# Fourteen stripes for a head, scatters at an even pace between gathers, dots that lag behind the heads

## The chip, the cores and the metric

The kernel runs on one core of one Trainium2 chip. The metric is the time of one execution in device microseconds (us); less is better.

## The reference, cut to what matters

One step of a decoder layer for 512 prompt tokens and 64 sample tokens, width 2048. After three branches (pooling, attention, cross-attention) and their merge comes the part that matters here, a feed-forward layer of 16384 experts of which each token uses 128:

```python
q = (xt @ w_q).reshape(n, PEER_HEADS, 2, PEER_HALF)
s = jnp.einsum('nhpd,hpkd->nhpk', q, subkeys)
s_top, i_top = lax.top_k(s, PEER_TOPK)
cand = s_top[:, :, 0, :, None] + s_top[:, :, 1, None, :]
cand_idx = i_top[:, :, 0, :, None] * PEER_N_KEYS + i_top[:, :, 1, None, :]
best, sel = lax.top_k(cand.reshape(n, PEER_HEADS, PEER_TOPK * PEER_TOPK), PEER_TOPK)
eidx = jnp.take_along_axis(cand_idx.reshape(n, PEER_HEADS, -1), sel, axis=-1)
gate = jax.nn.softmax(best, axis=-1)
...
a = jax.nn.gelu(jnp.einsum('ted,td->te', u[ib], xb), approximate=False)
return jnp.einsum('te,ted->td', gb * a, v[ib])
```

There are 8 heads (PEER_HEADS), 16 experts for each token and head (PEER_TOPK), 128 keys on each side (PEER_N_KEYS). `u` and `v` are the arrays `peer_u` and `peer_v`, 16384 rows of 2048.

## The kernel before

The kernel is a sequence of stages with a barrier between them. The change touches the one that reads `peer_u` (semaphores `q6`). The 576 tokens are five blocks: four of 128, one of 64. Blocks 1 to 3 (384 tokens) are treated densely: TensorE multiplies them by all of `peer_u`, in 128 stripes of 128 experts (kind "u"), ScalarE takes Gelu of each stripe's result and stores it in DRAM. Which experts a token has chosen is brought in by scatters: for each token, head and place, its gate goes to the place of (expert, token) in `routes_scratch`, which was filled with zeros earlier. Blocks 0 and 4 are treated sparsely: for each place, a gather brings 128 rows of `peer_u` (8 KB each, 1.05 MB a gather) into one of three buffers (`ring`), and VectorE forms the dot product of each row with its token in one instruction (`dot`, L1523). There are 192 gathers and 192 dots, and 384 scatters of 128 single values.

The queries of the heads come from 16 stripes of `w_pq` (kind "q", two a head, all 576 tokens in two column halves). So the stage has 144 stripes. They go in groups: the first GROUP x 8 stripes are 8 groups of two "q" and GROUP - 2 "u" stripes, and the rest are "u".

What each engine does for a stripe s:

- SyncE loads its two halves (512 KB each) into `w_raw`, four buffers, each when VectorE is done with the one before in that buffer.
- ScalarE rounds each half to fp32r (`w_hi`, L130). VectorE forms the rest (`w_lo`, L139); two such instructions a stripe are called its splits. There are four such pairs of buffers, two stripes of them.
- TensorE multiplies three times for each 128 x 128 block: hi by hi, lo by hi, hi by lo. A "u" stripe has 48 matmuls of 384 columns, a "q" stripe 96 of 288. After the third stripe of a group it also computes the head's scores.
- ScalarE drains the result (L1353 for "u", L1345 for "q"), so the starts of its drains mark the ends of stripes. After the fourth stripe of a group it copies the scores out.
- VectorE, after its splits of stripe s, does the steps that `plan` has for s, then dots up to `dots_by(s)`.

The steps of a head, all on VectorE: five `list` steps (top 16 of each side, a block each), `candidates`, `choose` (top 16 of the candidates), `shift`, `unpack`, two `look_up`, `number` (the expert's number), `weigh` (gates, and the copy `gate_sums` for the scatters), and `add_same(h)`. The last adds to a gate the gates of the same expert in earlier heads, in up to three parts of three heads each: a comparison (L1489), a product (L1491), a sum (L1493) and an addition (L1494). When it is done, `s_head` rises, and GpSimd may scatter and gather for that head. Nearly every step is a chain whose links wait for each other through `s_tk`.

VectorE's order is written out: HEAD_STEPS says in which stripe, counted from the head's first, a step stands (FIRST_STEPS for head 0). Before, with GROUP = 10, steps of head h reach into group h + 1: `add_same` is in the same stripe as the next head's `list1`.

GpSimd issues all gathers (L1325) and scatters (L1313) in one order: ahead of gather q it issues scatters until `scatters_before(q)` are out. Gather q waits until dot q - 3 is done (three buffers) and at every 24th for its head; the first scatter of a head waits for the head and for all scatters before it to land. ScalarE moves the sample tokens' part of `eidx` and `gate` to other partitions after each head (`move_sample`), and the gathers for sample tokens wait for that.

The stage ends when all dots, stores and scatters are done. Then the next stage multiplies by `peer_v`.

## Time and profile before

| what | us |
|---|---|
| median of three executions | 4664.35 (4663.63 to 4670.29) |
| the profiled execution | 4673.19 |
| its span | 4671.6 |
| matmul, busy | 4274.8 (92%) |
| VectorE, busy | 2644.5 (57%) |
| ScalarE, busy | 1249.9 (27%) |
| GpSimd, busy | 1715.3 (37%) |
| granted TensorE clock, mean | 0.954 |

The span reaches from the first to the last instruction of the profile, and all times of rows are counted from its start. Busy time of GpSimd is that in which it makes the descriptors of its DMAs, not that of the transfers. Shares are means over the stages; the stage of the change lies between 2051 and 3554 us.

### The profile page before, as it was taken

How to read it: one execution, taken by the hardware profiler on the slowest of the kernel's cores; microseconds unless marked ns; L12 is line 12 of the kernel's file. 1: busy time of each engine (PE TensorE's matmuls, PEld its weight loads, DVE VectorE, ACT ScalarE, POOL GpSimd, SP SyncE). 2: the span in 40 equal slices, each digit the busy share in tenths (PEclk: the TensorE clock that was granted, in tenths of full speed). 3: DMA queues.
4: the chain of work that ended last, by engine and by line, in shares of the span. 5: the costliest groups of instructions: out<-in, count | busy, mean ns of one | idle time of the engine just before them, and what ended most of it. 6: DMA issues, size and time to landing. Idle time of an engine off the chain costs nothing. (4 is left out here: it accounts for less than half of the span.)

```text
span 4671.6 us, 76860 instructions
## 1 busy us (share of the span) xinstructions
PE 4274.8 (92%) x28688; PEld 4161.8 (89%) x28688; DVE 2644.5 (57%) x3611; ACT 1249.9 (27%) x1625; POOL 1715.3 (37%) x1305
## 2 busy tenths in 40 slices
PE   5999999999698898969999998888886999999997
PEld 5999999999466798969999997888886999999997
DVE  4222111111322452246888889666666988888887
ACT  4111133333112221132333322222222333332332
POOL 0000100000111000002555544887785767666772
PEclk8999999999798999989999998999998999999998
DMA  4822332322476333135666655998887999999996
GB/s 158 314 81 81 124 107 104 107 104 90 142 253 256 139 133 129 63 123 178 245 245 222 216 215 217 331 335 317 319 314 289 372 361 357 359 356 362 358 355 258
DMA packets 279277, 1061.58 MB, mean 227 GB/s; under 512 B 43635, under 2 KB 94195, under 8 KB 225971
## 3 DMA queue, kind: packets, MB, share of 16 engines
q1 hardware_dynamic: 165490, 522.72, 31.1%
q0 software_dynamic: 93728, 510.53, 28.9%
q10 hardware_dynamic: 19936, 26.78, 1.6%
q8 instruction: 67, 1.10, 0.1%
q14 instruction: 56, 0.45, 0.0%
HBM read 977.47 MB, written 81.33 MB: 227 GB/s over the span
## 5 line engine op out<-in xcount | busy, mean ns | idle before, releaser
L139 DVE TENSOR_TENSOR w_lo<-w_raw,w_hi 128x1024 fp32r<-128x1024 f32 x498 | 600.8, 1230 | 1058.9 <-ACT w_hi L130 1048.7
L130 ACT ACTIVATE w_hi<-w_raw 128x1024 fp32r<-128x1024 f32 x498 | 519.2, 1059 | 1252.3 <-PE acc L167 760.0
L1313 POOL DMA_INDIRECT routes_scratch<-gate_sums,route x384 | 560.9, 1461 | 272.5 <-DVE gate_sums L1477 124.7
L167 PE MATMUL acc<-x_hi,w_hi 128*128 128x288 f32 x2592 | 558.0, 297 | 17.8 <-DVE w_lo L139 17.6
L167 PE MATMUL acc<-x_lo,w_hi 128*128 128x288 f32 x2592 | 557.3, 297 | 0.0
L167 PE MATMUL acc<-x_hi,w_lo 128*128 128x288 f32 x2592 | 556.9, 297 | 0.1
L167 PE MATMUL acc<-h_hi,w_hi 128*128 128x384 f32 (+1 forms) x1280 | 411.5, 338 | 98.2 <-DVE w_lo L139 96.4
L167 PEld LDWEIGHTS acc<-x_hi,w_hi 128*128 128x128 f32 x2592 | 419.8, 190 | 18.8 <-DVE w_lo L139 14.3
L167 PE MATMUL acc<-h_hi,w_hi_peeru 128*128 128x384 f32 (+1 forms) x1280 | 408.3, 335 | 30.6 <-DVE w_lo_peeru L139 30.6
L167 PEld LDWEIGHTS acc<-x_hi,w_lo 128*128 128x128 f32 x2592 | 419.7, 190 | 0.2 <-issue 0.2
L167 PEld LDWEIGHTS acc<-x_lo,w_hi 128*128 128x128 f32 x2592 | 419.9, 190 | 0.0
L167 PE MATMUL acc<-h_lo,w_hi 128*128 128x384 f32 (+1 forms) x1280 | 408.2, 335 | 0.0
L167 PE MATMUL acc<-h_hi,w_lo 128*128 128x384 f32 (+1 forms) x1280 | 407.3, 335 | 0.4 <-issue 0.4
L167 PE MATMUL acc<-h_lo,w_hi_peeru 128*128 128x384 f32 (+1 forms) x1280 | 406.0, 333 | 0.0
L167 PE MATMUL acc<-h_hi,w_lo_peeru 128*128 128x384 f32 (+1 forms) x1280 | 405.8, 333 | 0.0
L1796 PE MATMUL acc<-tile_hi,w_hi 128*128 128x384 f32 x1024 | 342.9, 335 | 45.8 <-DVE w_lo L139 45.8
L1523 DVE SCALAR_TENSOR_TENSOR ring<-ring,h_row 128x2048 f32<-128x2048 f32 x128 | 292.5, 2287 | 138.9 <-DMA ring<-in_peer_u,eidx 124.2
L130 ACT ACTIVATE w_hi_peeru<-w_raw 128x1024 fp32r<-128x1024 f32 x272 | 278.7, 1054 | 325.0 <-PE acc L1796 262.8
L139 DVE TENSOR_TENSOR w_lo_peeru<-w_raw,w_hi_peeru 128x1024 fp32r<-128x1024 f32 x272 | 322.1, 1224 | 68.6 <-ACT w_hi_peeru L130 50.1
L1796 PE MATMUL acc<-tile_hi,w_hi_peeru 128*128 128x384 f32 x1024 | 346.8, 339 | 0.2 <-DVE w_lo_peeru L139 0.2
L1796 PE MATMUL acc<-tile_lo,w_hi_peeru 128*128 128x384 f32 x1024 | 346.7, 339 | 0.0
L1796 PE MATMUL acc<-tile_hi,w_lo_peeru 128*128 128x384 f32 x1024 | 346.6, 338 | 0.0
(321 smaller groups left out, 8500.5 us busy)
## 6 DMA issues: line engine op xcount, KB each, us to landing
w_raw<-in_w_peer_u SPq DMA_DIRECT2D x256, 512.0 KB
w_raw<-in_w_peer_v SPq DMA_DIRECT2D x256, 512.0 KB
w_raw<-in_w_gate SPq DMA_DIRECT2D x96, 512.0 KB, 3.7
w_raw<-in_w_z SPq DMA_DIRECT2D x66, 512.0 KB, 3.3
k_ring<-in_cache_k SPq DMA_DIRECT2D x64, 512.0 KB, 5.0
v_ring<-in_cache_v POOLq DMA_DIRECT2D x64, 512.0 KB, 6.3
routes_scratch<-zero POOLq DMA_DIRECT2D x8, 3072.0 KB, 50.1
activations_scratch<-a_out ACTq DMA_DIRECT2D x128, 192.0 KB
```

Source lines behind the costliest of these rows:

```text
L130: nc.scalar.activation(slot(q, j)[0], raw[:, j % 4, :], ACT.Copy).then_inc(q["hi"], 1)
L139: nc.vector.tensor_tensor(lo, raw[:, j % 4, :], hi.bitcast(F32), ALU.subtract).then_inc(q["lo"], 1)
L167: last = nc.tensor.matmul(dst, l_, r_[:, cc, c0:c0 + cn], start=(cc == first and p_ == 0), stop=(cc == last_c and p_ == 2))
L1313: pool.indirect_dma_start(route_dram, bass.IndirectOffsetOnAxis(ap=route[:, b, n:n + 1], axis=0), gsum[:, h % SUMS, b - 1, n % PTOP:n % PT ...
L1523: nc.vector.scalar_tensor_tensor(out=ring[:, r, :], in0=ring[:, r, :], scalar=1.0, in1=hrow[:] if r < 2 else hrow_s[:], op0=ALU.mult, op1= ...
L1796: last = nc.tensor.matmul(acc[:, s, h, 0:ND], l_, r_[:, t_, :], start=(c == 0 and p_ == 0), stop=(c == GRP - 1 and p_ == 2))
```

## The change

A group has fourteen stripes instead of ten, so the 16 "q" stripes spread over 112 stripes instead of 80. HEAD_STEPS is laid out anew: `choose` goes block by block in five steps (before: three steps for blocks 0 and 1, 2 and 3, and 4), and `add_same` becomes three steps, one a part, `sums0` and `sums1` in stripe 16 and `sums2` in stripe 17 from the head's first, which are the third and fourth of the next group, where no `list` step stands. `s_head` then rises by an instruction of its own behind `sums2`. The dots start at stripe 16 instead of 14 and go at 1 a stripe to stripe 34, 7/5 a stripe to stripe 118, and 11/5 a stripe from there. In a stripe, half of its dots (rounded down) stand ahead of the head's steps. Ahead of gather q there are 9q/4 scatters, up to all 384; before, 3 a gather and 4 ahead of the first, to gather 70, and then 17/12 a gather.

```diff
-        GROUP = 10
+        GROUP = 14
...
-                      10: ("choose1",), 11: ("choose2", "shift"), 12: ("unpack", "look_up0"), 13: ("look_up1",), 14: ("number", "weigh"), 15: ("add_same",)}
...
+                      10: ("choose1", "choose2"), 11: ("choose3", "choose4", "shift"), 12: ("unpack",), 13: ("look_up0",), 14: ("look_up1",),
+                      15: ("number", "weigh"), 16: ("sums0", "sums1"), 17: ("sums2",)}
...
-        move_at = {s + 1: h for s in plan for h, name in plan[s] if name == ("add_same" if h else "weigh")}
-        LAST_STEP = GROUP * (PH - 1) + 14
+        move_at = {s + 1: h for s in plan for h, name in plan[s] if name == ("sums2" if h else "weigh")}
+        LAST_FREE = GROUP * (PH - 1) + 20
 
         def dots_by(s):
 
-            return 0 if s < 14 else min(NGAT, s - 13 if s < LAST_STEP else LAST_STEP - 13 + 2 * (s - LAST_STEP))
+            if s < 16:
+                return 0
+            return s - 15 if s <= 34 else min(NGAT, 19 + 7 * (min(s, LAST_FREE) - 34) // 5 + 11 * max(0, s - LAST_FREE) // 5)
 
         def scatters_before(q):
 
-            return 4 + 3 * q if q < 70 else min(NSCT, 214 + (q - 70) * 170 // 120)
+            return min(NSCT, 9 * q // 4)
...
-                def choose(blocks):
-                    link(sixteen([(cand[:, b, :], rest_c[:, n, :], best[:, b, :], sel[:, b, :]) for n, b in enumerate(blocks)]))
+                def choose(b):
+                    link(sixteen([(cand[:, b, :], rest_c[:, b % 2, :], best[:, b, :], sel[:, b, :])]))
...
-                def add_same(h):
-
-                    dve.wait_ge(s_lst, NBLK * (h + 1) + (h < PH - 1))
-                    for h0 in range(0, h, 3):
+                def add_same(h, part_no):
+
+                    h0 = 3 * part_no
+                    if h0 == 0 and h < PH - 1:
+                        dve.wait_ge(s_lst, NBLK * (h + 1))
+                    if h0 < h:
...
-                        last = nc.vector.tensor_tensor(gsum[:, h % SUMS], gsum[:, h % SUMS], psum_[:], ALU.add)
-                        if h0 + 3 < h:
-                            link(last)
-                    last.then_inc(s_head, 1)
+                        link(nc.vector.tensor_tensor(gsum[:, h % SUMS], gsum[:, h % SUMS], psum_[:], ALU.add))
+                    if part_no == 2:
+                        dve.sem_inc(s_head, 1)
...
                 for s in range(NS_):
                     split_lo(dve, s // 2, s % 2, q6)
+                    if s == 13:
+                        dve.wait_ge(s_hmv, 16)
+                    early = dots_by(s - 1) + (dots_by(s) - dots_by(s - 1)) // 2
+                    for q in range(dots_by(s - 1), early):
+                        dot(q)
                     for h, name in plan.get(s, ()):
                         step(h, name)
-                    if s == 13:
-                        dve.wait_ge(s_hmv, 16)
-                    for q in range(dots_by(s - 1), dots_by(s)):
+                    for q in range(early, dots_by(s)):
                         dot(q)
```

## Rows read from the trace of the kernel before

**Rows 1.** Windows cut at drains: bounds and length, busy time (instructions), clock, DMA share, GB/s.
```profile
2067.20:2149.50 82.30, 82.30 (x502) 82.30 (x501) 44.70 (x153) 28.11 (x35) 0.00 (x0) 1.00 0.40 132
2149.50:2849.40 699.90, 673.60 (x4173) 671.79 (x4172) 584.49 (x1326) 202.35 (x249) 351.68 (x280) 0.98 0.63 226
2247.30:2342.30 95.00, 95.00 (x598) 95.00 (x597) 80.37 (x193) 29.27 (x36) 51.22 (x40) 1.00 0.67 236
2437.40:2534.50 97.10, 95.29 (x598) 94.97 (x597) 84.56 (x193) 29.29 (x36) 51.63 (x41) 1.00 0.65 233
...
2742.50:2849.40 106.90, 97.02 (x597) 96.70 (x597) 93.00 (x197) 29.29 (x36) 47.91 (x40) 0.95 0.59 211
2849.40:2891.40 42.00, 42.00 (x243) 42.00 (x242) 37.65 (x55) 15.38 (x19) 19.29 (x13) 1.00 0.72 259
2891.40:3508.70 617.30, 531.10 (x2832) 522.08 (x2830) 417.04 (x364) 145.56 (x176) 491.44 (x284) 0.93 0.86 313
```

**Rows 2.** Waits, 2891.4 to 3508.7 us: us in total, times, longest.
```profile
DVE ring L1523 <- DMA ring<-in_peer_u,eidx: 121.9, 52, 7.9
...
DVE ring L1523 <- DMA ring<-in_peer_u,expert_sample: 60.3, 25, 5.7
```

**Rows 3.** GpSimd's groups by line, 2891.4 to 3508.7: busy us, mean ns | idle before.
```profile
L1313 POOL DMA_INDIRECT routes_scratch<-gate_sums,route x166 | 288.7, 1739 | 64.4 <-issue 57.4 <-DMA routes_scratch<-gate_sums,route 7.0
L1325 POOL DMA_INDIRECT ring<-in_peer_u,eidx x78 | 132.8, 1702 | 29.9 <-issue 22.6 <-DVE ring L1523 7.3
L1325 POOL DMA_INDIRECT ring<-in_peer_u,expert_sample x40 | 74.9, 1872 | 31.9 <-DVE ring L1523 20.3 <-issue 11.6
```

**Rows 4.** The same groups, 2240.9 to 2843.1 us.
```profile
L1313 POOL DMA_INDIRECT routes_scratch<-gate_sums,route x180 | 229.6, 1276 | 72.2 <-issue 53.6 <-DMA routes_scratch<-gate_sums,route 18.6
L1325 POOL DMA_INDIRECT ring<-in_peer_u,eidx x40 | 52.0, 1301 | 148.4 <-DVE ring L1523 145.6 <-issue 2.7
L1325 POOL DMA_INDIRECT ring<-in_peer_u,expert_sample x21 | 27.7, 1318 | 76.6 <-DVE ring L1523 75.4 <-issue 1.2
```

**Rows 5.** Timelines of GpSimd and VectorE, 2928 to 2950 us: start, us, instruction.
```profile
2931.30 2.73 POOL L1325 DMA_INDIRECT ring<-in_peer_u,eidx  x1 [0.30 <-issue]
2934.34 1.99 POOL L1313 DMA_INDIRECT routes_scratch<-gate_sums,route  x1 [0.30 <-issue]
...
2944.19 0.98 POOL L1325 DMA_INDIRECT ring<-in_peer_u,expert_sample  x1 [0.30 <-issue]
...
2930.90 2.29 DVE L1523 SCALAR_TENSOR_TENSOR ring<-ring,h_row 128x2048 f32<-128x2048 f32 x1 [3.31 <-DMA ring<-in_peer_u,eidx]
...
2933.11 2.36 DVE L139 TENSOR_TENSOR w_lo<-w_raw,w_hi 128x1024 fp32r<-128x1024 f32 x2
...
2944.35 2.29 DVE L1523 SCALAR_TENSOR_TENSOR ring<-ring,h_row 128x2048 f32<-128x2048 f32 x1 [1.31 <-DMA ring<-in_peer_u,eidx]
```

**Rows 6.** Timeline of VectorE over one stripe with a list and a dot.
```profile
2812.49 2.35 DVE L139 TENSOR_TENSOR w_lo<-w_raw,w_hi 128x1024 fp32r<-128x1024 f32 x2
...
2817.51 2.27 DVE L1523 SCALAR_TENSOR_TENSOR ring<-ring,g_row 128x2048 f32<-128x2048 f32 x1
...
2819.70 2.35 DVE L139 TENSOR_TENSOR w_lo_peeru<-w_raw,w_hi_peeru 128x1024 fp32r<-128x1024 f32 x2
```

**Rows 7.** VectorE's groups by line and form, 2040 to 3560 us.
```profile
L1489 DVE TENSOR_TENSOR same_expert<-eid_f,eidx 128x2304 f32<-128x2304 f32 x7 | 17.9, 2552 | 0.1
...
L1489 DVE TENSOR_TENSOR same_expert<-eid_f,eidx 128x768 f32<-128x768 f32 x3 | 2.9, 956 | 0.1
```

**Rows 8.** Window of VectorE over five stripes from `candidates` to `look_up1`: length, busy.
```profile
2834.80:2879.60 44.80, 39.75 (x78) 1.00 0.73 262
```

**Rows 9.** A window of the next stage, columns as in rows 1.
```profile
3700.00:3800.00 100.00, 100.00 (x573) 100.00 (x573) 89.70 (x80) 30.08 (x36) 68.23 (x51) 1.00 0.95 369
```

**Rows 10.** Timelines of VectorE, ScalarE and SyncE's queue at the end of the stage.
```profile
3515.44 2.29 DVE L1523 SCALAR_TENSOR_TENSOR ring<-ring,g_row 128x2048 f32<-128x2048 f32 x1 [1.07 <-DMA ring<-in_peer_u,expert_sample]
...
3508.69 0.49 ACT L1353 ACTIVATE a_out<-acc 128x384 f32<-128x384 f32 x1 [7.99 <-PE acc L167]
...
3519.47 0.40 SPq L1629 DMA_DIRECT2D out_t<-activations_scratch  x1
```

More of the change, by code:

```diff
@@ L1249, in build @@
         HEAD_STEPS = {4: ("list0",), 5: ("list1",), 6: ("list2",), 7: ("list3",), 8: ("list4",), 9: ("candidates", "choose0"),
-                      10: ("choose1",), 11: ("choose2", "shift"), 12: ("unpack", "look_up0"), 13: ("look_up1",), 14: ("number", "weigh"), 15: ("add_same",)}
-        FIRST_STEPS = {4: ("list0", "list1"), 5: ("list2", "list3"), 6: ("list4", "candidates"), 7: ("choose0",), 8: ("choose1",),
-                       9: ("choose2", "shift"), 10: ("unpack", "look_up0"), 11: ("look_up1", "number"), 12: ("weigh",)}
+                      10: ("choose1", "choose2"), 11: ("choose3", "choose4", "shift"), 12: ("unpack",), 13: ("look_up0",), 14: ("look_up1",),
+                      15: ("number", "weigh"), 16: ("sums0", "sums1"), 17: ("sums2",)}
+        FIRST_STEPS = {4: ("list0", "list1"), 5: ("list2", "list3"), 6: ("list4", "candidates"), 7: ("choose0", "choose1"),
+                       8: ("choose2", "choose3"), 9: ("choose4", "shift"), 10: ("unpack", "look_up0"), 11: ("look_up1", "number"), 12: ("weigh",)}
         plan = {}
@@ L1504, in step @@
                     elif name.startswith("choose"):
-                        choose(((0, 1), (2, 3), (4,))[int(name[6:])])
+                        choose(int(name[6:]))
                     elif name == "shift":
@@ L1516, in step @@
                     else:
-                        add_same(h)
+                        add_same(h, int(name[4:]))
                 def dot(q):
```

## The prediction

> **What bounds the kernel now.** I first asked the windows where TensorE is not full. Only the stage of the diff matters: it runs from about 2051 us to the first matmul of the next stage at 3554 us, and in it the windows are cut at the drains of single stripes [rows 1]. From 2067.2 to 2149.5 us nine stripes pass (one of kind "q", eight of kind "u", one set of scores) and TensorE is 100% busy; the five "u" stripes of 2849.4 to 2891.4 us take 42.0 us. So a "u" stripe costs 8.4 us, and a group of ten (two "q", eight "u", one set of scores) 95.0 us, as in the full window from 2247.3 us. Everything above that is lost time, and it stands in two places. The seven groups of 2149.5 to 2849.4 us take 699.9 us where 665.0 would do: 34.9 us. Their windows one by one (two that repeat the pattern aren't shown, 102.6 and 105.4 us) put 32.0 of it on the sums of heads 3 to 6 (2.1, 7.6, 10.4, 11.9) and nearly all the rest, 2.8, on the first. The last 59 stripes take 617.3 us where 495.6 would do: 121.7 us. Together 156.6 us, the most that a better order of this stage can give back.
>
> What ends last in each? In the last 59 stripes the waits [rows 2] say that VectorE stood 182.2 us for rows of `peer_u` to land, while GpSimd, which orders those transfers, stood only 27.6 us for a free buffer [rows 3]: GpSimd never catches up, its orders are the bottleneck. The groups by line give 284 orders (118 gathers, 166 scatters), busy 496.4 us with 126.2 us between them: 2.19 us an order, 2.07 without the 34.6 us in which it waited for a dot or a landing. In the early part [rows 4] 241 orders take 309.3 us, 1.28 us each, and 0.30 us stands between two that follow on each other: 1.58. The timelines of both engines [rows 5] show why one work has two prices. An order issued while VectorE is idle, as at 2944.19 us, takes 0.98 us. That of 2931.30 us takes 2.73: VectorE's dot ended at 2933.19 and the order 0.84 us behind it. That of 2934.34 met two splits that ended at 2935.47 and was done 0.86 us later. So an order waits for the end of a dot or split. The 0.98 us and the 0.30 us make a floor of 1.28 us.
>
> In heads 3 to 6 the loss is VectorE's. A stripe with one split pair, one list and one dot takes it 7.2 us, from 2812.49 to 2819.70 [rows 6]: 2.3 the pair, 2.2 the dot, 2.7 the list. `add_same` adds three steps of 2.55 us and some small change, 8.0 us, for three earlier heads, and 3.2 for one (three of 0.96) [rows 7]; I take 5.6 between them for two. All of it stands in the stripe of `list1`: 12.8 us for head 2 (loss 0.1), 15.2 for head 3 (2.1), 18.4, 20.8, 23.2 for heads 4 to 6 (7.6, 10.4, 11.9). About 13 us pass unseen since splits are ahead of TensorE; head 7's stripe (no list, but a second dot and three parts: 26 us) lies in the last window, and by the same slope I put 15 of its 121.7 us down to it.
>
> **The change, part by part.** *Work.* Nothing is removed: 192 gathers, 384 scatters and all vector steps remain, in another order. `choose` goes block by block, five chains of four links in place of three; the rows show no cost beyond some 0.1 us a link, under 1 us a head, hidden in stripes of 8.4 us. The added semaphore step on VectorE is an order of its sequencer. `move_sample` moves to the stripe after `sums2` with both its transfers and the sample gathers that wait for them; the first gather of a head is due later than that.
>
> *Pace.* Before, 71 dots were done at stripe 84 and then two a stripe. After: one a stripe to 34 (19 dots), 7/5 to 118 (136), then 11/5 (191 at stripe 143). A group of 14 costs TensorE 95.0 + 4 x 8.4 = 128.6 us, 9.19 a stripe.
>
> *Waits on heads.* Scatters of head h start before gather 22, 44, 65, 86, 107, 129, 150 (h = 1 to 7), which the dots let go at stripes 35, 51, 66, 81, 96, 112, 124; the heads are done at 31, 45, 59, 73, 87, 101, 115. Four to eleven stripes of margin: nothing, and a head must be 34 us late before GpSimd stands.
>
> *Sums.* `sums0` and `sums1` stand in the third stripe of the next group, behind two "q" stripes. 82.3 - 8 x 8.4 = 15.1 us is one "q" and the scores, 95.0 - 8 x 8.4 = 27.8 two and the scores: a "q" stripe takes TensorE 12.7 us, 4.3 more than "u", so about 17.3 us pass unseen there. With the dots of those stripes VectorE needs 17.9 us (head 4, two dots), 18.1 (head 5), 20.5 (head 6): 1 us and 4 us lost. Head 7 has no "q" stripes after it: 22.7 us against 13, by the losses above some 11, and 2 for the look-ups just before. Sum 18 us, where it was 32.0 + 15.
>
> *Stripes 34 to 118.* Each wants 1.4 x 3.25 = 4.55 orders. At the early 1.58 us that is 7.2 us of 9.19 (loss 0), at 2.07 it is 9.4, at 2.19 10.0, a loss of 0.8 x 84 = 65 us. VectorE: five stripes of choosing and look-ups are 39.75 us busy [rows 8], less five of (2.3 + 2.2), 17.3; with five lists of 2.7 that is 31 us over ten "u" stripes; with 1.4 dots and the splits 8.5 us a stripe against 8.4. So it has no room to wait for a gather, but the ring holds three rows, the head steps between dots are mostly short, and the "q" stripes give some 8 us a group back. I take 15 us, nearer the early row since its mix of steps is the same; ends 0 and 65.
>
> *Stripes 118 to 134.* Gathers 139 to 170 come with the last 72 scatters: 104 orders in the 134.4 us that 16 stripes need. Before, a gather took 617.3 / 118 = 5.23 us, of which 2.41 x 1.28 = 3.08 is the floor; the other 2.15 is held up by a dot and half a pair of splits (3.5 us of VectorE): 61% of it. After, a gather has 3.39 us of dot and splits beside it, 2.07 held up, and 3.25 x 1.28 = 4.16: 6.23 us, times 32 is 199 us. With 5 us for the last landing (an estimate) the loss is 70 us. Ends: 0 (104 x 1.28 = 133 us) and 98 (2.19 an order).
>
> *Stripes 134 to 144.* One order a gather, but 2.2 x 1.05 (128 rows of 2048 f32) + 1.05 (weights) + 0.2 = 3.55 MB a stripe; at the 369 GB/s of the next stage [rows 9] 9.6 us against 8.4. 10 us; ends 0 and 29 (at the 313 GB/s of the last window, [rows 1]).
>
> *The end.* Before, the last drain is at 3508.7, VectorE's last dots stand for rows until 3517.7, and the next stage's first load goes out at 3519.5 [rows 10]. After, three dots and no scatter are left in place of five: 6 us less (0 to 8); the last activation still has to be stored.
>
> *Sum.* Lost after: 2.8 + 18 + 15 + 70 + 10 = 115.8 us against 156.6: 40.8 us gained, with the end 47. The profiled execution took 4673.2 us (span 4671.6), 8.8 above the median of 4664.35; taken off the median, 4617 us.
>
> A rule to weigh here: the Trainium skill, SBUF — State Buffer, Who interferes with whom, says that a VectorE instruction with two SBUF inputs and a GpSimd one that reads SBUF lock each other out, and that issue order decides who waits. The first half agrees with [rows 5]. By the second, a dot or split that comes up while an order is under way would wait for it, half of its 0.98 us on average; with two such meetings a stripe that is 1 us a stripe from 34 to 118, where VectorE has none to spare, so some 80 us in place of 15. The trace does not bear it out: the dot of 2944.35, begun 0.16 us after an order, took its usual 2.29 [rows 5].
>
> **The rivals.** *Slower:* orders have the late price throughout, because 1.4 dots a stripe lay a dot or split over most of them. One price p for both stretches costs (4.55p - 9.19) x 84 + 104p + 5 - 134.4, which with the other 30.8 us passes the old 156.6 and the 6 of the end from p = 2.13 us an order. At 2.07 it gives 4637, at 2.19 some 4690. For it: 2.19 is what the late rows show. Against: that has 34.7 us of waits in it, and in the early rows the orders fall among lists.
>
> *VectorE is full* in stripes 34 to 118, so a dot's wait for its row goes to the end. Before, 119 late dots waited 1.5 us each. At 0.6 us for 117 dots, in ten of 14 stripes, 50 us in place of 15: 4652; at 0.75, 4662, no change. For it: 8.5 against 8.4 us. Against: before, early dots had their rows at once. *Orders hold up dots,* the mutual lock: each meeting costs VectorE half an order, 84 us in place of 15: 4686; against it stands the dot of 2944.35 [rows 5]. It is the second half of the rule in that section of SBUF — State Buffer of the Trainium skill.
>
> *Scatters spread out cost little:* while VectorE stands for a row, orders run at the floor. At 1.6 us an order the dense stretch loses 37 us and the earlier none: 68 in all, 4570; at the floor 4532.
>
> *The change does nothing:* the late stretch is paced by bytes, 313 GB/s there [rows 1]. Against: 369 with TensorE full in the next stage [rows 9]. 4664.
>
> **How the numbers follow.** Forecast (4580 to 4645): 0.57. Much faster, around 4550: 0.14. VectorE full, around 4655: 0.12. Slower by dear orders, 4675 to 4690: 0.11; by orders that hold up dots: 0.02. Nothing: 0.04. 0.2% is 9.3 us, about what a measurement of this kernel tells from no change. Faster by more: 0.57 + 0.14 + 0.04 of the VectorE case = 0.75; within: 0.09; slower: 0.16. The range leaves out the far half of the fast and of the slow cases, 4565 to 4675; the forecast's own is 4590 to 4645.
>
> **What would show it.** Right: groups of 14 near 129 us up to head 5 and 5 us or less over it at head 6; a loss of some 13 us behind stripe 114; then sixteen stripes that take about 200 us with VectorE waiting for rows, GpSimd hardly ever; then ten of about 9.5 us; drains end near 3468. Wrong: groups of 135 us or more with waits for rows in them; orders above 2.1 us from stripe 34 on; or the dense stretch at TensorE's pace. The weakest number is the 70 us, since it extends a share of held-up time to a density of scatters that no row shows.

## The result and the profile after

The changed kernel takes **4593.09 us**, the median of 4 runs (4578.19 to 4604.84), against 4664.82 (4663.63 to 4670.29) for the kernel before on the same chip: ratio 0.9848, 95% interval 0.983 to 0.9866. That is 71.7 us off the median where 47 were forecast. The profiled run is the slowest of the four (4604.84 us, span 4603.3), and against the profiled run of before it is 68.4 us shorter, so the traces are compared on those 68 us: 2.0 because the stage starts earlier (first drain at 2065.2 us, not 2067.2; nothing ahead of it was edited), 60.3 inside the stage (1381.2 us from first to last drain, not 1441.5), 7.6 at its end, and 1.6 given back in the rest of the program.

The windows of the changed kernel, cut at the drains of stripes 0, 34, 97, 110, 118, 134 and 143, are the answer to [rows 1]. Columns as there.

```profile
2065.20:2379.50 314.30, 314.30 (x1934) 314.30 (x1933) 201.66 (x471) 96.37 (x119) 80.39 (x70) 1.00 0.60 205
2379.50:2953.00 573.50, 573.50 (x3490) 573.50 (x3489) 524.56 (x991) 177.62 (x216) 447.26 (x280) 1.00 0.84 292
2953.00:3081.10 128.10, 123.00 (x742) 122.81 (x742) 117.03 (x218) 36.85 (x46) 98.02 (x63) 0.97 0.80 281
3081.10:3163.80 82.70, 69.98 (x386) 69.67 (x385) 71.33 (x66) 19.99 (x25) 64.09 (x38) 0.92 0.77 268
3163.80:3363.90 200.10, 152.18 (x768) 148.40 (x766) 110.31 (x97) 39.94 (x48) 162.12 (x108) 0.89 0.80 270
3363.90:3446.40 82.50, 77.77 (x432) 77.14 (x432) 67.20 (x61) 20.93 (x25) 28.36 (x19) 0.98 0.96 374
```

TensorE is busy for the whole length of the first two: in 97 stripes the head steps, and in the last 63 of them 1.4 dots and 3.15 scatters a stripe, cost it nothing. What is lost stands in the last four. A "u" stripe is 8.4 us, so 16 take 134.4 and nine 75.6, and the table compares each stretch with the terms of the prediction.

| stretch | us lost, forecast | us lost, measured |
|---|---|---|
| first group | 2.8 | 0 |
| sums of heads 1 to 6 | 5 (1 and 4) | 7.8, all of it head 6 |
| head 7, behind stripe 114 | 13 | 15.6 |
| waits in stripes 34 to 118 | 15 | 0 apart from head 6's row |
| stripes 118 to 134 | 70 | 65.7 (200.1 - 134.4) |
| stripes 134 to 143 | 10 | 6.9 (82.5 - 75.6) |
| sum, where before it was 156.6 | 115.8 | 96.0 |

In the dense stretch, 3163.8 to 3363.9 us, the waits of VectorE answer to [rows 2] (us in total, times, longest):

```profile
DVE ring L1527 <- DMA ring<-in_peer_u,eidx: 51.4, 16, 6.7
...
DVE ring L1527 <- DMA ring<-in_peer_u,expert_sample: 38.9, 10, 7.3
```

and GpSimd's groups by line over the same stretch to [rows 3]:

```profile
L1316 POOL DMA_INDIRECT routes_scratch<-gate_sums,route x74 | 110.7, 1495 | 27.1 <-issue 22.3 <-DMA routes_scratch<-gate_sums,route 4.8
L1328 POOL DMA_INDIRECT ring<-in_peer_u,eidx x23 | 32.7, 1421 | 7.0 <-issue 7.0
L1328 POOL DMA_INDIRECT ring<-in_peer_u,expert_sample x11 | 19.3, 1753 | 3.4 <-issue 3.4
```

VectorE stands 90.3 us for rows, and GpSimd, which orders them, never once for a dot: its idle time is all issue and 4.8 us of a landing. 108 orders in 200.1 us are 1.85 us each; 34 of them are gathers, 5.89 us each (6.23 forecast), of which 1.28 x 108 / 34 = 4.07 is the floor and 1.82 is held up (2.07 forecast). The timelines of GpSimd and of VectorE in that stretch show the holding up as [rows 5] did:

```profile
3270.59 0.97 POOL L1316 DMA_INDIRECT routes_scratch<-gate_sums,route  x1 [0.30 <-issue]
3271.86 2.88 POOL L1328 DMA_INDIRECT ring<-in_peer_u,eidx  x1 [0.30 <-issue]
```

```profile
3271.59 2.29 DVE L1527 SCALAR_TENSOR_TENSOR ring<-ring,g_row 128x2048 f32<-128x2048 f32 x1 [3.44 <-DMA ring<-in_peer_u,expert_sample]
```

The order at 3270.59 us met an idle VectorE and took 0.97 us. The next met the dot that ran to 3273.88, and was done at 3274.74, 0.86 behind it.

Of the 65.7 us TensorE stands 47.9. In the other 17.8 it works, but slower: its 768 matmuls are busy 152.2 us at a granted clock of 0.89, where the same number takes 134.4 at 1.00. After a wait of 9.59 us they begin 0.32 us apart, in the full stretches 0.17 to 0.18:

```profile
3287.53 0.68 PE L167 MATMUL acc<-h_hi,w_hi_peeru 128*128 128x384 f32 x1 [9.59 <-DVE w_lo_peeru L139]
3288.01 0.52 PE L167 MATMUL acc<-h_lo,w_hi_peeru 128*128 128x384 f32 x1
```

The granted clock over 3286.5 to 3298.8 us is 0.72, so part of that time is at 1.2 GHz and part at 2.4. As GpSimd never waits for VectorE or TensorE here, this is how TensorE's loss is made up and not a second cause of the stretch's length.

In the last nine intervals the picture turns round:

```profile
L1328 POOL DMA_INDIRECT ring<-in_peer_u,eidx x12 | 17.0, 1419 | 31.6 <-DVE ring L1527 31.3 <-issue 0.3
L1328 POOL DMA_INDIRECT ring<-in_peer_u,expert_sample x7 | 11.3, 1618 | 18.2 <-DVE ring L1527 18.2
```

Here GpSimd is idle 49.5 of 82.5 us for want of a free buffer, and the DMA engines are busy 0.96 of the time at 374 GB/s (windows above). That points to bytes, but does not show that they set the pace: e1 below moves 406 GB/s with the same gathers and weights. These 49.5 us next to a stretch in which GpSimd is the bottleneck are what the later experiments try to use.

The end of the stage answers to [rows 10]: the last dot, the last drain and the next stage's first load.

```profile
3445.84 2.29 DVE L1527 SCALAR_TENSOR_TENSOR ring<-ring,g_row 128x2048 f32<-128x2048 f32 x1 [2.96 <-DMA ring<-in_peer_u,expert_sample]
3446.41 0.49 ACT L1356 ACTIVATE a_out<-acc 128x384 f32<-128x384 f32 x1 [7.99 <-PE acc L167]
...
3449.90 0.40 SPq L1636 DMA_DIRECT2D out_t<-activations_scratch  x1
```

The dots now end 2 us behind the last drain and no longer 9, so the load goes out 3.5 us behind it, where it was 10.8. That is the gain at the end: the next stage's first matmul stands 38.1 us behind the last drain, where it was 45.8.

### The profile page after: what moved, and what is told of

It is laid out like the page before. It is cut to its first block and busy times, and to the rows that moved or that the text cites. A ratio compares the mean times of both kernels' runs of the same rounds, so it can differ in the third digit from the quotient of the medians.

```text
span 4603.3 us, 76657 instructions
## 1 busy us (share of the span) xinstructions
PE 4257.1 (92%) x28688; PEld 4150.7 (90%) x28688; DVE 2650.1 (58%) x3611; ACT 1250.6 (27%) x1625; POOL 1737.1 (38%) x1305
## 5 line engine op out<-in xcount | busy, mean ns | idle before, releaser
L1316 POOL DMA_INDIRECT routes_scratch<-gate_sums,route x384 | 584.1, 1521 | 145.1 <-issue 114.9
L167 PE MATMUL acc<-x_hi,w_hi 128*128 128x288 f32 x2592 | 557.5, 297 | 18.6 <-DVE w_lo L139 18.6
L167 PE MATMUL acc<-h_hi,w_hi 128*128 128x384 f32 (+1 forms) x1280 | 400.9, 330 | 30.5 <-DVE w_lo L139 30.5
L1803 PE MATMUL acc<-tile_hi,w_lo 128*128 128x384 f32 x1024 | 342.7, 335 | 0.0
```

The lines of the kernel that those rows point to most:

```text
L167: last = nc.tensor.matmul(dst, l_, r_[:, cc, c0:c0 + cn], start=(cc == first and p_ == 0), stop=(cc == last_c and p_ == 2))
L1316: pool.indirect_dma_start(route_dram, bass.IndirectOffsetOnAxis(ap=route[:, b, n:n + 1], axis=0), gsum[:, h % SUMS, b - 1, n % PTOP:n % PT ...
L1803: last = nc.tensor.matmul(acc[:, s, h, 0:ND], l_, r_[:, t_, :], start=(c == 0 and p_ == 0), stop=(c == GRP - 1 and p_ == 2))
```

## The experiments

Losses are worked out as above, stretch by stretch, from the drains of each profiled run. They carry the comparison better than whole spans do: the first drain of the stage moved between 2055.1 and 2067.2 us over the profiled runs, though no kernel here edits anything ahead of it. "The change" is the changed kernel; its 96.0 us are the measure.

**e1: the dense stretch without its scatters.**

```diff
-        NGAT, NSCT = NEXP + HC, 3 * NEXP
+        NGAT, NSCT = NEXP + HC, 3 * NEXP - 72
```

> The changed kernel without its last 72 scatters (their gates never reach the routes, so that part of the output is left out); the gathers and dots stay. Theory (the dense stretch of stripes 118 to 134 is set by the number of GpSimd's orders): with one order a gather it runs like stripes 134 to 143 do now, 82.5 us for nine, 9.2 us each, so 16 stripes take about 147 us in place of 200, and the time falls by about 50 us to some 4540 us. Rival (the stretch is set by bytes, or by VectorE and its dots): the scatters are only bystanders, the stretch keeps 180 us or more and the time stays within 15 us of 4593.

Measured: 4538.27 us (4520.91 to 4542.34), ratio 0.9735 (0.9719 to 0.9751). Stripes 118 to 134 and 134 to 143:

```profile
3147.80:3285.30 137.50, 134.78 (x770) 134.15 (x769) 113.63 (x101) 40.03 (x49) 54.84 (x37) 1.00 1.01 406
3285.30:3364.00 78.70, 75.75 (x432) 75.11 (x430) 63.42 (x57) 20.59 (x25) 29.14 (x18) 1.00 0.96 377
```

65.7 us of loss become 3.1, in the same stretch with the same gathers, dots and weights. The rate rises from 270 to 406 GB/s, so the bytes did not pace it. VectorE's waits for rows fall from 90.3 to 24.1 us, and GpSimd, which never stood for a dot, now stands 80.7 us for free buffers. So the scatters make the loss; that it is their orders, and not their transfers, e2 shows. The profiled run is the fastest of its four, 17 us below their median; by the medians this kernel is 55 us faster than the change.

**e2: dots with one SBUF input.**

```diff
-                    nc.vector.scalar_tensor_tensor(out=ring[:, r, :], in0=ring[:, r, :], scalar=1.0, in1=hrow[:] if r < 2 else hrow_s[:],
-                                                   op0=ALU.mult, op1=ALU.mult, accum_out=dots[:, c:c + 1]).then_inc(s_used, 1)
+                    nc.vector.reduce_sum(dots[:, c:c + 1], ring[:, r, :], AX.X).then_inc(s_used, 1)
```

> The changed kernel with each dot replaced by a plain sum of the gathered row (one SBUF input in place of two; the product with the token is left out). Theory (an order waits for the end of a VectorE instruction with two SBUF inputs): orders that come under a dot fall from about 2.2 us to 1.0, a gather with its 2.25 scatters costs 3.25 x 1.28 = 4.2 us and half a pair of splits, about 4.9 us in place of 6.2, stripes 118 to 134 take about 155 us in place of 200, and the time falls by about 40 us to 4550. Rival (orders are slow because queues and transfers are busy, whatever VectorE does): orders stay at 1.5 us on average and the time within 10 us of 4593, as far as the sum takes as long as the dot did (2.2 us).

Measured: 4544.79 us (4541.46 to 4547.73), ratio 0.9747 (0.973 to 0.9763). Window, GpSimd's groups and VectorE's group of dots in stripes 118 to 134:

```profile
3153.20:3308.70 155.50, 140.27 (x769) 138.68 (x768) 113.51 (x67) 40.22 (x48) 110.86 (x106) 0.96 0.96 352
```

```profile
L1316 POOL DMA_INDIRECT routes_scratch<-gate_sums,route x72 | 76.6, 1063 | 28.3 <-issue 21.6 <-DMA routes_scratch<-gate_sums,route 6.7
L1328 POOL DMA_INDIRECT ring<-in_peer_u,eidx x22 | 21.9, 997 | 9.2 <-issue 5.8 <-DVE dots L1527 3.4
```

```profile
L1527 DVE TENSOR_REDUCE dots<-ring 128x1 f32<-128x2048 f32 x35 | 79.8, 2284 | 38.9 <-DMA ring<-in_peer_u,eidx 23.3 <-DMA ring<-in_peer_u,expert_sample 15.4
```

The reduction takes VectorE as long as the dot did, 2284 against 2293 ns, and all orders are still there. A scatter falls from 1495 to 1063 ns, the stretch from 200.1 to 155.5 us (155 expected). The edit takes two things away: the second input, and the writing of the whole product back over the row, since a reduction writes one value a partition. One pair of timelines shows both sides: first an order that lies whole inside a reduction and takes its 0.98 us, then one that meets the splits, which still have two inputs, and takes 1.69.

```profile
3224.02 0.98 POOL L1328 DMA_INDIRECT ring<-in_peer_u,eidx  x1 [0.31 <-issue]
...
3226.60 1.69 POOL L1316 DMA_INDIRECT routes_scratch<-gate_sums,route  x1 [0.30 <-issue]
```

```profile
3224.02 2.29 DVE L1527 TENSOR_REDUCE dots<-ring 128x1 f32<-128x2048 f32 x1 [4.19 <-DMA ring<-in_peer_u,expert_sample]
3226.23 2.35 DVE L139 TENSOR_TENSOR w_lo_peeru<-w_raw,w_hi_peeru 128x1024 fp32r<-128x1024 f32 x2
```

Which of the two it is can be read from the changed kernel's own trace. The next stage adds a result in PSUM to one in SBUF and writes all of it to SBUF (`out_t`):

```profile
3662.87 0.56 DVE L1780 TENSOR_TENSOR out_t<-acc,out_t 128x384 f32 x1 [1.24 <-PE acc L1803]
3662.98 1.00 POOL L1691 DMA_INDIRECT ring_v<-in_peer_v,expert_stage  x1 [0.81 <-POOL expert_stage L1688]
```

Sixteen orders of that trace were begun with more than 0.3 us of such an addition left, and none took over 1.01 us; held until 0.85 us behind it, this one would have taken 1.3. Of 140 orders begun with as much left of a dot, all ended 0.80 to 0.87 us behind it. So the held-up part of an order belongs to VectorE instructions that read two SBUF operands, not to the writing, as the prediction's model had it and as the first half of the rule in the Trainium skill, SBUF — State Buffer, Who interferes with whom, has it. The same section infers that a `tensor_tensor` does not hold back the making of descriptors. The splits are `tensor_tensor` instructions and do hold it back, 1.69 us instead of 0.98 above, and the measurement decides.

**e3: the sums with the second list, as before.** They stand in stripe 19 of a head, where no "q" stripe follows.

```diff
-                      15: ("number", "weigh"), 16: ("sums0", "sums1"), 17: ("sums2",)}
+                      15: ("number", "weigh"), 19: ("sums0", "sums1", "sums2")}
...
-                        dve.wait_ge(s_lst, NBLK * (h + 1))
+                        dve.wait_ge(s_lst, NBLK * (h + 1) + 1)
```

> The changed kernel with all three parts of the sums back in the stripe of the next head's second list, as before the change. Theory (what the new place is worth is the 4.3 us that each of two q stripes gives VectorE as a lead): the sums of heads 3 to 6 lose again what they lost before or a little more for the second dot, 2, 8, 10 and 12 us or so, where now they lose 0, 0, 0 and 8; head 7 loses 17 in place of 15.6. Sum some 25 to 30 us slower than the change, about 4620 us. Rival (the place does not matter, longer groups alone give the lead back before the sums come): the time stays within 8 us of 4593.

Measured: 4638.53 us (4633.54 to 4648.66), ratio 0.9944 (0.9926 to 0.9961). Three stretches of 14 stripes, each 128.6 us without loss, and the dense stretch:

```profile
2462.60:2593.50 130.90, 129.04 (x791) 128.72 (x790) 112.32 (x218) 39.35 (x49) 96.55 (x65) 1.00 0.82 290
...
2593.50:2731.10 137.60, 131.62 (x790) 130.61 (x789) 117.03 (x220) 39.24 (x48) 99.27 (x66) 0.98 0.80 279
2731.10:2872.10 141.00, 132.61 (x790) 131.97 (x789) 117.72 (x222) 39.31 (x49) 94.89 (x63) 0.96 0.75 263
...
3208.70:3407.50 198.80, 151.06 (x768) 147.26 (x766) 107.85 (x95) 39.93 (x48) 159.58 (x107) 0.89 0.80 271
```

The dense stretch and what follows are within 2 us of the change. Up to stripe 118 this kernel loses 69.6 us where the change loses 23.4: 46 us, the whole distance of the medians. I had priced the place of the sums at 25 to 30, from the 47 us of before less 18. That was too little, because heads 2 to 6 lose 2.1, 2.3, 7.6, 12.6 and 12.2 us at the sums themselves, head 7 loses 19.3 (I had put 15 down to it), and 10.5 more go eight stripes behind the sums of heads 3 and 4 (drains 70 and 84). With 1.4 dots a stripe VectorE, busy for 117 us and more in such a group, has less room to catch up than it had before. The edit moves the sums away from the "q" stripes, but it also puts all three parts in one stripe and beside a `list` of 2.7 us. The 46 us are the price of all of this together; what the "q" stripes alone are worth no run separates.

**e4: the pace alone.** Groups of ten and the head steps of before, with the dots and scatters of the change.

The edit is shown against the kernel before.

```diff
-            return 0 if s < 14 else min(NGAT, s - 13 if s < LAST_STEP else LAST_STEP - 13 + 2 * (s - LAST_STEP))
+            if s < 16:
+                return 0
+            return s - 15 if s <= 34 else min(NGAT, 19 + 7 * (min(s, 118) - 34) // 5 + 11 * max(0, s - 118) // 5)
...
-            return 4 + 3 * q if q < 70 else min(NSCT, 214 + (q - 70) * 170 // 120)
+            return min(NSCT, 9 * q // 4)
...
+                    early = dots_by(s - 1) + (dots_by(s) - dots_by(s - 1)) // 2
+                    for q in range(dots_by(s - 1), early):
+                        dot(q)
                     for h, name in plan.get(s, ()):
                         step(h, name)
...
-                    for q in range(dots_by(s - 1), dots_by(s)):
+                    for q in range(early, dots_by(s)):
                         dot(q)
```

> The kernel before, groups of ten and its head steps untouched, with only the new pace of dots and scatters. Theory: stripes 118 to 143 lose about 73 us as in the change, stripes 84 to 118 lose nothing at 1.4 dots; the groups of ten lose the 32 + 15 us of the sums as before, and 10 to 20 us more because VectorE with 1.4 dots has 88 to 104 us of work in a group of 95. In all 130 to 140 us lost in the stage where it was 157 and is 96: about 4630 us. Rival (all of the gain is the pace): the time is that of the change, 4593. Other rival (nothing of it is): 4664.

Measured: 4651.91 us (4633.6 to 4661.97, 10 runs), ratio 0.9978 (0.9964 to 0.9991): 11 us faster than before where 33 were expected. Two groups of ten (95.0 us without loss) and the dense stretch:

```profile
2428.50:2529.30 100.80, 96.79 (x598) 96.47 (x598) 94.67 (x207) 29.34 (x37) 73.20 (x47) 0.98 0.79 270
...
2740.60:2849.70 109.10, 97.08 (x598) 96.76 (x598) 101.60 (x207) 29.29 (x36) 73.10 (x46) 0.94 0.69 246
...
3205.40:3408.40 203.00, 153.00 (x768) 148.87 (x767) 112.05 (x99) 39.98 (x49) 165.67 (x109) 0.88 0.80 272
```

VectorE is busy for 101.6 us in a group that should take 95.0 in all: here it is full, as the rival had it. The groups lose 41.4 us where before lost 34.9, and 22.3 more go in the ten stripes with head 7's sums. The pace is worth what it saves late, and groups of ten have no room for the dots that it brings forward. The pace needs the rest of the change: 11 us for the pace alone, 25 for the pace in groups of 14 (e3), 69 to 72 for both with the sums behind "q" stripes. What groups of 14 give at the old pace was not tried.

**e5: one part of the sums a stripe.**

```diff
-                      15: ("number", "weigh"), 16: ("sums0", "sums1"), 17: ("sums2",)}
+                      15: ("number", "weigh", "sums0"), 16: ("sums1",), 17: ("sums2",)}
```

> The changed kernel with the three parts of the sums in stripes 15, 16 and 17 of a head, one each, so the first moves into a q stripe behind number and weigh. Theory (in the change heads 6 and 7 lose 7.9 and 15.6 us because stripe 16 holds 20.5 and 24.5 us of VectorE's work): head 6 loses nothing, as 9.9 + 8 us in a q stripe and 12.5 after it fit in the lead, head 7 some 4 to 8 us; the time falls by 15 to 20 us to about 4575. Rival (the sums as a whole overfill the group, wherever they stand): the loss moves to the next stripes and the time stays within 5 us of 4593.

Measured: 4596.32 us (4589.87 to 4596.94), ratio 0.9857 (0.9834 to 0.9881): no gain. Head 6 loses 1.6 us and head 7 14.7, now in two lumps of 7.3 and 7.5 where it was one of 15.6. At head 6 nothing is won either: e11, the change again, loses 1.0 us there. The run's rival holds, within 5 us of 4593: the loss of head 7 only moved. The expectation took the lump for the cause. Likely it is the sum, since the last "q" stripe is stripe 99 and no later stripe gives VectorE more room; in e10 a later place alone wins 5 us of such a loss.

**e6: the last scatters spread to the end.** GpSimd's 49.5 idle us in stripes 134 to 143 get 26 of the 74 scatters.

```diff
-            return min(NSCT, 9 * q // 4)
+            return 9 * q // 4 if q < 139 else min(NSCT, 312 + 18 * (q - 139) // 13)
```

> The changed kernel with the last 72 scatters spread evenly over gathers 139 to 191 (18/13 a gather) where they stood before gathers 139 to 170 (9/4). Theory (GpSimd's orders set the last 26 stripes, and after gather 170 it is idle half of the time): 125 orders at 1.85 us are 231 us where 26 stripes need 218, so the stretch loses 13 to 25 us in place of 72.6, and the time falls by about 50 us to 4545. Rival (with 2.2 gathers a stripe their bytes beside the scatters hold the end back as they do in the late stretch of the kernel before): the stretch keeps 50 us or more of its loss, about 4580.

Measured: 4590.8 us (4584.94 to 4594.44), ratio 0.985 (0.9826 to 0.9874), where 4545 were expected. Stripes 118 to 134 and 134 to 143, and GpSimd's groups over both (3155 to 3440 us):

```profile
3158.80:3330.80 172.00, 146.59 (x770) 144.06 (x769) 113.30 (x100) 39.98 (x48) 138.72 (x82) 0.92 0.89 320
3330.80:3423.50 92.70, 81.14 (x432) 79.55 (x431) 63.08 (x55) 20.48 (x25) 79.06 (x45) 0.94 0.87 312
```

```profile
L1316 POOL DMA_INDIRECT routes_scratch<-gate_sums,route x74 | 127.3, 1720 | 27.1 <-issue 22.3 <-DMA routes_scratch<-gate_sums,route 4.9
L1328 POOL DMA_INDIRECT ring<-in_peer_u,eidx x36 | 60.1, 1669 | 12.6 <-issue 10.7 <-DVE ring L1527 2.0
L1328 POOL DMA_INDIRECT ring<-in_peer_u,expert_sample x18 | 35.5, 1973 | 7.8 <-issue 5.2 <-DVE ring L1527 2.6
```

I had carried the 1.85 us an order of the change over to the new mix. But a scatter costs 1.72 us here and 1.50 there. The price that stays is another: 128 orders at the floor are 163.8 us, and what is left of 264.7 us over 54 gathers is 1.87 us a gather, against 1.82 in the change. GpSimd's time is 1.28 us an order and some 1.85 us a gather, since every gather brings a dot and half a pair of splits, and those hold up an order that is issued while they run. So both stretches together win 17.9 us of their 282.6, not 50. They keep 54.7 us of loss, as the rival had it (50 or more), but not for its reason: 320 and 312 GB/s are far below the 406 of e1. And 7.0 us of the gain go again at the end: with the buffers always late, the last gather is ordered 1.3 us ahead of the last drain (3422.2 us; in the change 7.9 ahead, at 3438.5), and the next stage's first matmul comes 45.1 us behind that drain instead of 38.1.

**e7: e5 and e6 together.**

```diff
-                      15: ("number", "weigh"), 16: ("sums0", "sums1"), 17: ("sums2",)}
+                      15: ("number", "weigh", "sums0"), 16: ("sums1",), 17: ("sums2",)}
...
-            return min(NSCT, 9 * q // 4)
+            return 9 * q // 4 if q < 139 else min(NSCT, 312 + 18 * (q - 139) // 13)
```

> Both edits of the two runs above together. Theory (the two losses lie in different stretches and add up): the stage loses about 20 to 35 us in all, and the time is near 4528 us. Rival (what is won before stripe 118 is waited away behind it): no faster than the better of the two alone, 4545.

Measured: 4578.74 us (4576.32 to 4586.87, 5 runs), ratio 0.9823 (0.9804 to 0.9842), 12 below e6 and 50 above what was expected, for the reasons of both.

**e8: more scatters early.** GpSimd gets 16 of the late scatters in stripes 34 to 118, where each order had 2.06 us of room.

```diff
-                      15: ("number", "weigh"), 16: ("sums0", "sums1"), 17: ("sums2",)}
+                      15: ("number", "weigh", "sums0"), 16: ("sums1",), 17: ("sums2",)}
...
-            return min(NSCT, 9 * q // 4)
+            return 12 * q // 5 if q < 139 else min(NSCT, 333 + (q - 139))
```

> As the run before, but 12/5 scatters a gather up to gather 139 and one a gather after it, so that stripes 34 to 118 carry 4.76 orders each in place of 4.55 and the last 26 only 104 in place of 125. Theory: up to stripe 118 an order has 2.06 us of room and takes 1.9, so 4.76 orders just fit in 9.19 us (9.0), and the end loses nothing by orders; 0 to 10 us faster than the run before, about 4520. Rival (stripes 34 to 118 are full already): they begin to lose, 20 us or more, and the time is above 4535.

Measured: 4564.45 us (4557.97 to 4571.42), ratio 0.9793 (0.9768 to 0.9818), 14 below e7. The late stretches lose 28.9 us (159.0 and 79.9 us), where e7 lost 49.3, and stripes 34 to 118 lose 30.0 where e7 lost 18.6. At 396 orders in that part GpSimd has 2.0 us each, and the dots wait 30.4 us for rows in it (22.8 and 7.6 by the two kinds of row), where in the change they wait 14.8. The dots are those of e7, and VectorE is busy 712.7 us there, in e7 710.8; so the 11 us more come with the orders, as far as one profiled run of each can tell. The rival, that these stripes are full already, was right.

**e9: more dots early.**

```diff
-            if s < 16:
+            if s < 14:
...
-            return s - 15 if s <= 34 else min(NGAT, 19 + 7 * (min(s, LAST_FREE) - 34) // 5 + 11 * max(0, s - LAST_FREE) // 5)
+            return s - 13 if s <= 34 else min(NGAT, 21 + 3 * (min(s, LAST_FREE) - 34) // 2 + 7 * max(0, s - LAST_FREE) // 4)
...
-            return min(NSCT, 9 * q // 4)
+            return 9 * q // 4 if q < 150 else min(NSCT, 337 + 6 * (q - 150) // 5)
```

> The changed kernel with the sums spread over stripes 15 to 17, dots from stripe 14, 3/2 a stripe in place of 7/5 from 34 to 118 (147 done there in place of 136) and 7/4 from 118, scatters 9/4 a gather up to gather 150 and 6/5 after it. Theory (GpSimd's time is 1.28 us for each order and 1.9 us more for each gather, wherever they stand): stripes 34 to 118 want 409 x 1.28 + 126 x 1.9 = 763 us of the 795 that they take, the last 26 want 89 x 1.28 + 42 x 1.9 = 194 of 218, so neither loses much; left are the 16 us of head 7's sums and some 15 us of uneven places: stage loss about 30 us in place of 96, time about 4530. Rival (VectorE, with 8.8 us a stripe of work between heads, is the next bound): stripes 34 to 118 lose 40 us or more and the time is no better than the 4564 of the run with 12/5 scatters.

Measured: 4567.05 us (4554.88 to 4570.09), ratio 0.9776 (0.9758 to 0.9795). Stripes 34 to 118, 118 to 134 and 134 to 143:

```profile
2380.70:3192.90 812.20, 776.40 (x4614) 771.59 (x4613) 729.24 (x1289) 234.26 (x286) 649.09 (x405) 0.98 0.82 288
3192.90:3337.90 145.00, 137.01 (x770) 136.23 (x769) 100.70 (x89) 40.04 (x49) 108.89 (x65) 0.98 0.93 343
3337.90:3413.50 75.60, 75.60 (x432) 75.27 (x430) 56.73 (x50) 20.46 (x25) 49.91 (x29) 1.00 0.90 332
```

The end of the stage is clean, and the loss has moved forward: 51.3 of 62 us lie ahead of stripe 118. VectorE's waits for rows ahead of stripe 118, first of the change and then of e9 (us in total, times, longest):

```profile
DVE ring L1527 <- DMA ring<-in_peer_u,eidx: 11.8, 7, 4.7
DVE ring L1527 <- DMA ring<-in_peer_u,expert_sample: 3.0, 3, 1.6
```

```profile
DVE ring L1527 <- DMA ring<-in_peer_u,eidx: 22.0, 17, 2.0
DVE ring L1527 <- DMA ring<-in_peer_u,expert_sample: 21.7, 9, 4.0
```

14.8 us have become 43.7, and VectorE, busy 729.2 of 812.2 us, has little slack for them. By the numbers the rival holds (40 us or more, no better than 4564). That a full VectorE is the cause is not shown. The expectation had set 763 us of GpSimd's orders against 795, but TensorE needs only 760.6 us for these stripes, so by its own price GpSimd was full too: 405 orders are busy 649.1 us with 119.6 between them, 768.7 in all (in the change 722.8, in e8 748.2). Both engines are at their limit, and no run separates them.

**e10: e9 with the second and third part of head 7's sums a stripe later.** They had lost 16.8 us in e9, at drains 113 to 115.

```diff
+        LAST_STEPS = {**HEAD_STEPS, 16: (), 17: ("sums1",), 18: ("sums2",)}
...
-            for r, names in (HEAD_STEPS if h else FIRST_STEPS).items():
+            for r, names in (LAST_STEPS if h == PH - 1 else HEAD_STEPS if h else FIRST_STEPS).items():
```

> As the run before, but head 7, behind which no q stripes come, has its second and third part of the sums in stripes 17 and 18 in place of 16 and 17. Theory: of the 15 us that they lose there some 5 to 7 are won, time about 4524. Rival (the sums overfill the last group as a whole): within 4 us of the run before.

Measured: 4562.87 us (4557.82 to 4572.78, 5 runs), ratio 0.9781 (0.9765 to 0.9797). Those drains lose 11.6 us now, but the whole is 4 us below e9 and within the spread of both. e8, e9 and e10 are the fastest versions, and their intervals overlap.

**e11: the change again,** with no edit, on the same chip as e9 and e10, to see what its spread is made of.

> The changed kernel once more, for its time beside the others of this call and for a second profile. Theory: about 4593 us; stripes 34 to 118 lose 8 and 13 to 16 us at heads 6 and 7 as in the first profile and nothing else, while the dense stretch of 118 to 134, where GpSimd and VectorE wait for each other, differs by 5 us or more from the 65.7 of the first: the spread of its times (26 us over four executions, the kernel before 7) comes from there. Rival: it comes from stages that the change does not touch.

Measured: 4601.18 us (4597.85 to 4602.1), ratio 0.9856 (0.9841 to 0.9871); e10 is 38 us below it. Stripes 34 to 97, 118 to 134 and 134 to 143:

```profile
2379.00:2953.00 574.00, 573.85 (x3490) 573.53 (x3490) 524.48 (x991) 177.67 (x217) 446.41 (x282) 1.00 0.83 292
3157.20:3358.40 201.20, 153.93 (x768) 150.15 (x767) 109.23 (x96) 39.95 (x48) 163.06 (x108) 0.87 0.79 269
3358.40:3441.60 83.20, 78.47 (x432) 78.16 (x432) 68.42 (x61) 20.50 (x25) 30.60 (x19) 0.96 0.95 371
```

All stretches repeat to about 1 us but one: head 6 loses 1.0 us here and 7.8 in the first profiled run. The dense stretch, where the expectation had looked for 5 us or more, differs by 1.1. VectorE's timelines there, first of the change and then of e11, show why.

```profile
2970.26 2.29 DVE L1527 SCALAR_TENSOR_TENSOR ring<-ring,h_row 128x2048 f32<-128x2048 f32 x1 [4.68 <-DMA ring<-in_peer_u,eidx]
...
2974.75 2.55 DVE L1494 TENSOR_TENSOR same_expert<-eid_f,eidx 128x2304 f32<-128x2304 f32 x1
```

```profile
2965.88 2.29 DVE L1527 SCALAR_TENSOR_TENSOR ring<-ring,h_row 128x2048 f32<-128x2048 f32 x1
...
2970.38 2.55 DVE L1494 TENSOR_TENSOR same_expert<-eid_f,eidx 128x2304 f32<-128x2304 f32 x1
```

One dot waited 4.68 us for its row, the sums began 4.4 us later, and TensorE lost 6.8 us more behind them. Over the two stripes in question (drains 99 to 101, 118 matmuls in both runs) it stood 5.1 us at a granted clock of 0.87, in e11 0.8 us at 1.00; the matmuls were busy 21.8 us, in e11 19.3. So 4.3 us of the 6.8 are the wait and 2.5 the slower clock around it. Why the row was late in one run and not in the other stays open, and so does the rest of the spread of 4578 to 4605 us: some of it is upstream of the stage, some is such single waits.

## Why the prediction was right, and where it was off

The direction, the mechanism and the range held; the point, 4617 us, was 24 too slow. Step by step:

- **What bounds each part.** Right: late, GpSimd's orders (e1 takes 72 of them away and 62.6 of 65.7 us go, 55 by the medians), held up by two-input instructions of VectorE (e2); early, the sums.
- **Stripes 34 to 118: 15 us.** This is the step that failed, "I take 15 us": it was 0 in e11, and in the first profiled run the 6.8 us that the table has under head 6. The price of an order was not the early row's 1.58 us either: 380 orders are busy 1.61 us each, 1.91 with the 0.30 between two. It still fitted, since the stripes need 760.6 us without loss (not 84 x 9.19 = 772: they hold five pairs of "q" stripes and not six) and leave each order 2.00. The waits of the dots came to 14.8 us in ten pieces, and TensorE lost nothing to them save where one stood in front of head 6's sums. e9 shows how near the edge is: 0.1 dot a stripe more, with 25 orders more, and these stripes lose 51 us where the change loses 23. Whether the full VectorE of that rival or the orders are behind it stays open.
- **Sums: 18 us.** Measured 23.4. Heads 1 to 5 cost nothing (1 forecast), head 6 1.0 to 7.8 (4), head 7 15.6 (13). The account of the "q" stripe, 4.3 us of room each, fits: the same sums in one stripe, beside a `list` and away from the "q" stripes, cost 46 us more (e3), though no run gives the part of the "q" stripes alone. What I had charged to the old place, 47 us for heads 3 to 7, would have been too little at the new pace.
- **Stripes 118 to 134: 70 us.** Measured 65.7, the best of the terms. The form of the sum (floor for each order, a held-up part for each gather) was right and the held-up part 0.25 us too large. The 2.15 us a gather that it started from held the 34.6 us in which GpSimd had waited for a dot or a landing; without them it is 1.86, close to the 1.82 and 1.87 measured since. That the term came within 5 us is in part luck: 34 gathers fell in the stretch and not 32. The 5 us for a landing, which no row ahead of the prediction shows, were 4.8. In e6 I forgot my own formula, used a price per order, and was 46 us out.
- **Stripes 134 to 143: 10 us.** Measured 6.9, at 374 GB/s where 369 were put in. The size fits, but that bytes make this loss is not shown: e1 moves 406 GB/s in the stretch before it.
- **First group: 2.8 us.** Measured 0. In e4, still in groups of ten, the first group loses 0.1, so it was the pace or the order in a stripe and not the length of the group.
- **The end: 6 us.** Measured 7.6, by the mechanism forecast.
- **Waits on heads: nothing.** Right: no scatter of these stretches waits for a head.
- **The rivals.** Orders at 2.13 us or more throughout: no, 1.91 in stripes 34 to 118 and 1.85 in the dense stretch. (At 2.19 us its formula gives 4696 us and not "some 4690".) Orders that hold up dots: no, 34 dots among 108 orders took a mean of 2.29 us. This is the second half of the rule in the Trainium skill, SBUF — State Buffer, Who interferes with whom, that issue order decides who blocks, and no run here bears it out for VectorE. Scatters that cost little: no, an order had 1.85 us in the dense stretch and not the 1.28 to 1.6 of that case. No effect: no; the dense stretch is not paced by bytes (e1).

Of the 21 us between forecast and profiled gain, the stage gave 19.5 (15 + 2.8 + 4.3 + 3.1 - 5.4, less 0.3 of rounding), the end 1.6, and the start and the rest of the program cancel. The last 3 us are the profiled runs': that of before lies 8.4 us above its median here, that of the change 11.8.

## What to carry to other kernels

Price a software-ordered transfer in two parts, a floor for each order and a held-up time for each two-input VectorE instruction that it can meet, and place orders so that this sum stays under TensorE's time in every stretch; an average price from one mix misleads in another. Put a lump of VectorE work where TensorE, which follows VectorE, is still in the stripes that take it longest, and let no wait for a transfer stand in front of it. When work is pushed towards the end of a stage, look at what the next stage's first load waits for, since there the last microseconds of a gain are given back.

## What the runs showed of the hardware

- A VectorE reduction over 128 x 2048 f32 took 2284 ns and the two-input multiply with accumulation over the same tile 2293, but only the second held up GpSimd's orders: 1.05 us an order among reductions, 1.50 among multiplies (means over 106 and 108 orders).
- An order begun while VectorE ran a dot ended 0.80 to 0.87 us behind it (140 of 140 in the changed kernel with more than 0.3 us of it left); under an addition with one input in PSUM none of 16 was held.
- The held-up time went with the number of gathers, not of orders: 1.82 us a gather at 3.2 orders each, 1.87 at 2.4.
- TensorE worked more slowly around its waits: of 65.7 us lost in the dense stretch 17.8 were matmuls that took longer, at a granted clock of 0.89.
- Without the scatters one core moved 406 GB/s over 137.5 us with TensorE at full clock and busy 98% of the time (e1).
- Work ahead of the stage, the same in all kernels, ended anywhere between 2055.1 and 2067.2 us in the profiled runs (first drain). What makes it vary was not tried.
